# Moving the 1024-column sum of weight blocks in paired w_out from VectorE to GpSimd

## What is computed

```python
for layer in range(DEPTH):
    h = rms_norm(x, norm_w[layer])
    proj = jnp.einsum('bsd,de->bse', h, w_in[layer])
    ...                      # four token mixers: GLA, sliding window, differential, RG-LRU
    y = jnp.concatenate([y_gla, y_swa, y_diff, y_lru], axis=-1)
    y = y * jax.nn.silu(gate)
    x = x + jnp.einsum('bse,ed->bsd', y, w_out[layer])
```

## Time and profile before

| | us |
|---|---|
| median of 3 runs | 2874.45 |
| lowest, highest | 2874.27, 2875.07 |
| the profiled execution | 2875.7 |
| its span, first to last instruction | 2874.0 |

### The profile page before, as it was taken

One profiled execution on the slowest core, in us unless ns is written; L12 is line 12 of the kernel. 1 busy time (PEld: TensorE's weight loads), 2 busy tenths in 40 slices (PEclk: granted clock), 3 DMA queues, 4 the chain that ended last, 5 costly groups with the idle time before them and its releaser, 6 DMA issues.

```text
span 2874.0 us, 35012 instructions
## 1 busy us (share of the span) xinstructions
PE 2860.9 (100%) x13317; PEld 2346.7 (82%) x13317; DVE 1837.1 (64%) x2428; ACT 1519.7 (53%) x2125; POOL 54.5 (2%) x90
## 2 busy tenths in 40 slices
PE   9999999999999999999999999999999999999999
PEld 7878888888888888888888788888888888888887
DVE  6545555555666568888864455555556665688888
ACT  6444445545556556555644345455556565564454
POOL 2000000000000000000000000000000000000000
PEclk9999999999999999999999999999999999999999
DMA  8655555666555665666676555565656556656665
GB/s 252 197 169 164 173 175 179 188 186 180 174 170 167 214 190 185 221 224 216 202 216 184 176 169 169 177 187 178 187 177 179 168 168 214 190 187 224 233 220 176
DMA packets 282873, 546.51 MB, mean 190 GB/s; under 512 B 17528, under 2 KB 22272, under 8 KB 282704
## 3 DMA queue, kind: packets, MB, share of 16 engines
q1 hardware_dynamic: 272848, 525.40, 59.0%
q0 software_dynamic: 5168, 16.73, 1.9%
q10 hardware_dynamic: 4688, 2.13, 0.3%
HBM read 535.81 MB, written 8.39 MB: 189 GB/s over the span
## 4 chain that ended last, share of the span: by engine, by line
PE 97%; DVE 1%; DMA 1%; issue 1%; ACT 0%; SPq 0%; DVEq 0%; ACTq 0%
PE main L1346 79%; PE mixer L1346 16%; DMA w_raw<-in_w_out 1%; PE mixer L1629 0%; DVE w_lo L839 0%; PE mixer L1387 0%; PE mixer L1376 0%; DVE mix L1119 0%; PE mixer L1565 0%; PE mixer L1608 0%; DVE w_lo L822 0%; ACT w_hi L598 0%; DMA w_raw<-in_w_in 0%; PE mixer L1593 0%; PE mixer L1481 0%
## 5 line engine op out<-in xcount | busy, mean ns | idle before, releaser
L1346 PE MATMUL main<-w_hi,act 128*128 128x512 f32 x6624 | 2134.7, 394 | 4.3 <-DVE act L811 1.4
L1346 PEld LDWEIGHTS main<-w_hi,act 128*128 128x128 f32 x6624 | 1244.7, 188 | 275.1 <-DVE w_lo L822 7.4
L822 DVE TENSOR_TENSOR w_lo<-w_raw,w_hi 128x1024 fp32r<-128x1024 f32 x736 | 895.1, 1228 | 758.4 <-ACT w_hi L457 754.5
L1346 PE MATMUL main<-w_lo,act 128*128 128x512 f32 x3312 | 1290.9, 390 | 0.0
L457 ACT ACTIVATE w_hi<-w_raw 128x1024 fp32r<-128x1024 f32 x736 | 770.6, 1057 | 559.1 <-PE main L1346 509.5
L1346 PEld LDWEIGHTS main<-w_lo,act 128*128 128x128 f32 x3312 | 623.2, 188 | 123.1
L598 ACT ACTIVATE w_hi<-w_raw 128x1024 fp32r<-128x1024 f32 x256 | 268.1, 1056 | 202.8 <-DVE w_raw L836 56.9
L839 DVE TENSOR_TENSOR w_lo<-w_raw,w_hi 128x1024 fp32r<-128x1024 f32 x256 | 307.9, 1220 | 34.5 <-ACT w_hi L598 30.6
L1346 PE MATMUL mixer<-w_hi,act 128*128 128x512 f32 x736 | 239.9, 389 | 0.0
L1346 PEld LDWEIGHTS mixer<-w_hi,act 128*128 128x128 f32 x736 | 138.1, 188 | 28.5
L1346 PE MATMUL mixer<-w_lo,act 128*128 128x512 f32 x368 | 143.2, 389 | 0.0
(11 more groups left out here) (267 smaller groups left out, 1667.4 us busy)
## 6 DMA issues: line engine op xcount, KB each, us to landing
w_raw<-in_w_in SPq DMA_DIRECT2D x736, 512.0 KB, 3.8
w_raw<-in_w_out SPq DMA_DIRECT2D x256, 512.0 KB, 4.3
out<-mix POOLq DMA_DIRECT2D x7, 1024.0 KB, 5.7
mix<-in_x POOLq DMA_DIRECT2D x4, 1024.0 KB, 6.8
mix<-out POOLq DMA_DIRECT2D x4, 1024.0 KB, 8.1
mix_Y<-in_x SPq DMA_DIRECT2D x7, 512.0 KB, 6.7
act_T<-in_lru_w_r ACTq DMA_DIRECT2D x16, 64.0 KB, 1.8
act_T<-in_lru_w_i ACTq DMA_DIRECT2D x16, 64.0 KB, 1.9
```

Of the source, the lines that this page charges most:

```text
L822: dve.tensor_tensor(w_lo[:, n % LO, :, :], w_raw[:, n % RAW, :, :], w_hi[:, n % HI, :, :].bitcast(F32), ALU.subtract).then_inc(w_lo_ready, 1)
L1346: return pe.matmul(out_, lhsT, rhs, start=start, stop=stop, skip_group_check=True)
```

## The change

L846 is taken out of VectorE's program and given to GpSimd as `block_sums`. GpSimd waits for the even block's landing and for b_raw[0] (b_sum at 2u + 2, u numbering the 48 fast places), makes the sum and raises b_pair. ScalarE's b_hi waits for b_pair, and for SP a fast place's even buffer is free when its own w_lo is made and b_pair is raised (`first_half`), in place of the wait for the odd slot's w_lo. On GpSimd the order of loads and stores of x changes: x pairs 0 and 1 are loaded ahead, a store comes at the start of the next x pair, and the load of x pair c + 1 behind the first sum of x pair c.

```diff
--- before.py
+++ after.py
@@ -206,7 +206,7 @@
         X_BANKS = (M[0], M[1], M[2], M[5])
         c_ready, p_done, p_added = sem("c_ready"), sem("p_done"), sem("p_added")
         s_sum, s_hi, s_ready = sem("s_summed"), sem("s_hi_ready"), sem("s_ready")
-        b_sum = sem("b_summed")
+        b_sum, b_pair = sem("b_summed"), sem("b_pair_summed")
         b_hi_ready, b_lo_ready, b_used = sem("b_hi_ready"), sem("b_lo_ready"), sem("b_used")
 
         block = ctx.enter_context(nc.Block())
@@ -254,10 +254,11 @@
 
         P_STEPS = 8
 
-        def read_raw(n):
-
-            s = n % (CHUNKS * NG) - J_OUT * NG
-            return n + 2 if s >= 0 and s % 2 == 0 and is_fast(s % 32) else n + 1
+        def first_half(n):
+
+            layer, s = divmod(n, CHUNKS * NG)
+            c, s = divmod(s - J_OUT * NG, 2 * NG)
+            return fast_number(layer, c, ORDER[s // 2]) if c >= 0 and s % 2 == 0 and is_fast(s) else None
 
         def y_scale(layer, k):
             return par[:, layer, Q_YS + k:Q_YS + k + 1]
@@ -278,7 +279,10 @@
                     col = (j - J_OUT + g % 2) * NC
                     src = w_out[layer, rows, col:col + NC]
                 if n >= RAW:
-                    sp.wait_ge(w_lo_ready, read_raw(n - RAW))
+                    sp.wait_ge(w_lo_ready, n - RAW + 1)
+                    u = first_half(n - RAW)
+                    if u is not None:
+                        sp.wait_ge(b_pair, u + 1)
                 sp.dma_start(w_raw[:, n % RAW, :, :], src.rearrange("(k p) n -> p k n", p=P)
                              ).then_inc(w_landed[n % RAW], 16)
 
@@ -388,6 +392,15 @@
                 pool.dma_start(out[0, :, 2 * c * NC:(2 * c + 2) * NC].rearrange("(t p) n -> p t n", p=P), x_pair[f % 2]
                                ).then_inc(x_stored, 16)
 
+            def block_sums(layer, c, g):
+
+                u = fast_number(layer, c, g)
+                n = pair_group(layer, c, 2 * ORDER.index(g))
+                pool.wait_ge(w_landed[n % RAW], 16 * (n // RAW + 1))
+                pool.wait_ge(b_sum, 2 * u + 2)
+                pool.tensor_tensor(b_raw[:, 1:3, :], w_raw[:, n % RAW, :, :],
+                                   b_raw[:, 0:1, :].to_broadcast([P, 2, NC]), ALU.add).then_inc(b_pair, 1)
+
             pool.wait_ge(w_used, 6)
             def rows(dst, src):
                 pool.dma_start(dst, src).then_inc(rows_in, 16)
@@ -410,11 +423,16 @@
                 for i in range(4):
                     mask_intra(layer, i)
                 load_x(layer, 0)
+                load_x(layer, 1)
                 for c in range(PAIRS):
-                    if c + 1 < PAIRS:
-                        load_x(layer, c + 1)
-                    if layer < LAST or c + 1 < PAIRS:
-                        store_x(layer, c)
+                    if c:
+                        store_x(layer, c - 1)
+                    for q, g in enumerate(FAST):
+                        block_sums(layer, c, g)
+                        if q == 0 and 0 < c < PAIRS - 1:
+                            load_x(layer, c + 1)
+                if layer < LAST:
+                    store_x(layer, PAIRS - 1)
                 if layer < LAST:
                     f = (layer + 1) * PAIRS
                     pool.wait_ge(x_stored, f * 16)
@@ -594,10 +612,10 @@
                 fast = is_fast(s) and s % 2
                 if fast:
                     u = fast_number(layer, c, ORDER[s // 2])
-                    act.wait_ge(b_sum, 3 * u + 1)
+                    act.wait_ge(b_sum, 2 * u + 1)
                 act.activation(w_hi[:, n % HI, :, :], w_raw[:, n % RAW, :, :], ACT.Copy).then_inc(w_hi_ready, 1)
                 if fast:
-                    act.wait_ge(b_sum, 3 * u + 3)
+                    act.wait_ge(b_pair, u + 1)
                     act.wait_ge(b_used, u)
                     act.activation(b_hi[:, :, :], b_raw, ACT.Copy).then_inc(b_hi_ready, 1)
 
@@ -839,12 +857,9 @@
                 dve.tensor_tensor(w_lo[:, n % LO, :, :], raw, w_hi[:, n % HI, :, :].bitcast(F32),
                                   ALU.subtract).then_inc(w_lo_ready, 1)
                 if fast and s % 2 == 0:
-                    dve.wait_ge(b_sum, 3 * u + 1)
+                    dve.wait_ge(b_sum, 2 * u + 1)
                     dve.wait_ge(b_used, u)
                     dve.tensor_tensor(b_raw[:, 0, :], second[:, 0, :], second[:, 1, :], ALU.subtract).then_inc(b_sum, 1)
-                    dve.wait_ge(b_sum, 3 * u + 2)
-                    dve.tensor_tensor(b_raw[:, 1:3, :], raw, b_raw[:, 0:1, :].to_broadcast([P, 2, NC]),
-                                      ALU.add).then_inc(b_sum, 1)
                 if fast and s % 2:
                     dve.wait_ge(b_hi_ready, u + 1)
                     dve.tensor_tensor(b_lo[:, :, :], b_raw, b_hi[:, :, :].bitcast(F32), ALU.subtract).then_inc(b_lo_ready, 1)
```

## The result

| | before | changed |
|---|---|---|
| median | 2874.43 us (4 runs) | 2949.97 us (4 runs) |
| lowest, highest | 2874.27, 2875.07 | 2949.64, 2951.11 |
| span of the profiled execution | 2874.0 | 2948.1 |
| ratio | | 1.0263 [1.0245, 1.0281] |

A forecast was written before the change was run, and what follows sets the result against it. TensorE was taken to bound the kernel (97% of the chain). Per x pair, first lateness plus periods' excess over 10.2 us minus slack summed to 64.2, less 2.6 existing waits: 62 us slower, 2936.5 us, range 2886 to 2972.

The forecast's parts named there:

- Step (b): Paired w_out fast places: GpSimd's sum takes 2.3 us, waits for the odd w_lo and ends 2.1 us later than before.
- Rival 1: Fast places: GpSimd does not wait for VectorE, the sum ends at 4.8, total 2889 us; chance 0.14.
- Step (c): Fast-place period: work queued behind the late sum makes it 11.3 us, 1.1 over TensorE's; 13.1 with an x load.
- rival 4: x load and both weights start together: perhaps 1 to 2 us more in four places, 4 to 8 us; no chance given.
- The move costs nothing else: Reordered x loads and stores: no cost beyond the x load's meeting with the weights, since their waits are done by then.
- The slack is won back between x pairs: Between x pairs of paired w_out: TensorE's lead of b_lo over its use recovers, as in the kernel before.
- waits already there: Paired w_out: 2.6 us that TensorE's weight loads already wait for b_lo, taken off the summed 64.2 us.
- ten regular places: Stretch between x pairs: said to be long enough to win the slack back.
- step d: x pair 0 of each layer, x pair 3 of layer 0: VectorE's split operations add 1.6 us a period.
- first lateness: First fast place of each x pair: the sum, and b_lo behind it, comes 2.1 us later.

The follow-up runs named there:

- e2: Changed kernel with VectorE's odd w_lo held back until GpSimd's sum is done; 2919.05 us, ratio 1.0147.
- e4: Changed kernel with the sum split, VectorE making the first 512 of 1024 columns and GpSimd the other 512; 2886.39 us, ratio 1.0038.
- e9: Changed kernel with the next regular slot's w_hi made before b_hi on ScalarE and its w_lo before b_lo on VectorE; 2936.56 us, ratio 1.0208.
- e10: e9 with, in addition, SP asking for the odd weight block of the next fast place first; 2904.08 us, ratio 1.0101.
- e13: Changed kernel with only the two weight loads of a fast place swapped, odd block first; 2940.80 us, ratio 1.0228.
- e1: Kernel before with only GpSimd's changed order of x loads and stores, the sum staying on VectorE; 2883.40 us, ratio 1.0022.
- e3: Kernel before with the 1024-column sum made twice in a row on VectorE; 2932.03 us, ratio 1.0192.
- e11: Kernel before with VectorE's three sums ahead of the even w_lo and the even block's successor asked for early; 2872.12 us, ratio 0.9985.
- e12: Kernel before with SP asking for the even block's successor when the sum is done, not the odd w_lo; 2873.82 us, ratio 0.9992.
- e5: Changed kernel with the load of the next x behind the last sum of an x pair, not the first; 2950.31 us, ratio 1.0261.

## Why the prediction was right, and where it missed

**Step (b), the sum's end: right.** I put it at 5.77 behind L836; it came at 5.80. GpSimd's work was 2.25 us behind the wait (taken: 2.2) and 2.40 alone (2.3); the odd w_lo started first, kept its 1.22 and held GpSimd up, as the earlier trace rows had shown. Rival 1 (no wait) needed 4.8. The sum was recorded from 0.23 behind the odd w_lo, where I had said 0.04 to 0.1, and with 3.24 us, just under the 3.3 to 3.4. e2, e4 and the reverse case in the changed kernel confirm the mechanism on both sides.

**Step (c), the period: right for plain ones, 11.3 and 11.30.** The bound was VectorE's queue, and the landing at about 10.8 lay just under it, as e9, e10 and e13 show. With an x load I took 13.1; the changed kernel has 13.70, 13.63, 13.77 and 13.96. The step's size was off by 0.5 to 0.9 in four places, 2.7 us: load and weights now start together, which is rival 4's case. I had priced it at 1 to 2 us a place, too high, and not put it into the sum.

**"The move costs nothing else": wrong.** The forecast did have the load meet the weights in x pairs 1 and 2 of layer 1, at 2.9 us each; e1, with the sum still on VectorE, has 2.3 and 2.6 there. What it did not have is that x pairs 2 and 3 then begin 1.1 and 2.7 us late. I argued from what each load waits for, and not from what it pushes back. My range for e1 left out even the part that the forecast had.

**The slack is won back between x pairs: wrong, above all in layer 1.** From the last fast place of one x pair to the last of the next, TensorE's first b_hi load fell further behind the kernel before by (us):

| | x pair 0 | 1 | 2 | 3 |
|---|---|---|---|---|
| layer 0, forecast | 8.7 | 7.0 | 7.0 | 13.6 |
| layer 0, measured | 7.5 | 8.5 | 8.8 | 11.7 |
| layer 1, forecast | 8.7 | 7.0 | 7.0 | 5.2 |
| layer 1, measured | 7.5 | 10.5 | 10.8 | 9.0 |

The measured ones add up to 74.2, the forecast's to 64.2, less 2.6 that I took off for waits already there. Errors of both signs are in it: x pair 0 of both layers and x pair 3 of layer 0 came out 4 us lower than forecast in all, the other five 14 us higher, and 11 of these lie in three x pairs of layer 1. I had used 2.4 us, the slack of x pair 1 of layer 0, for x pairs 1 and 2 of both layers and for x pair 3 of layer 1. The kernel before has next to no slack in x pair 1 of layer 1:

```profile
2637.93 1.76 DVE L850 TENSOR_TENSOR b_lo<-mix_Y,b_hi 128x1536 fp32r<-128x1536 f32 x1 [0.42 <-ACT b_hi L602]
```

```profile
2639.74 0.19 PEld L1346 LDWEIGHTS mixer<-b_hi,sums 128*128 128x128 f32 x1 [0.44 <-DVE b_lo L850]
```

b_lo ends at 2639.69, and TensorE has waited 0.44 us for it. In x pair 2 of layer 1 it is the same (0.05 us from b_lo's end to the load), and in x pair 3 the slack is 1.44. With these three values the forecast would have been 5.7 us higher; the x loads account for 1.5 more.

The sentence on the "ten regular places" that win the slack back is wrong too. Ten blocks lie there, which are five regular places (14, 15, 0, 1 and 2). With one fast place they are 47 products, and at 10.20 / 15 = 0.68 us each TensorE needs 31.96 us, which is the shortest that any run has there in layer 1. From the last fast place of one x pair to the first of the next the changed kernel takes 34.27, 35.24 and 35.38 us in layer 1, the kernel before 32.36, 32.80 and 31.96. The reorder of the loads is not needed for this: e3, which has the old order and a late sum, takes 34.51, 35.01 and 35.12. In that stretch VectorE of the changed kernel (x pair 1 to 2) stands idle for a landing:

```profile
2771.09 0.69 DVE L854 TENSOR_TENSOR w_raw<-w_raw 128x512 f32<-128x512 f32 x1 [4.95 <-DMA w_raw<-in_w_out]
```

TensorE has no transposes of x to make there in layer 1 (in layer 0 there are sixteen, L1387 in the kernel before, which its chain shows as two pieces of 0.87 us), so the weights' side, with a store of 1 MB beside its reload, has less time to recover: TensorE's own time there is 33.77 us in layer 0 and 31.96 in layer 1 (e11, e12). That these 1.8 us are the reason for the difference between the layers is argued, and was not tried; the rest of the 11 us stays open.

**Splits (step d): right in mechanism, high in effect.** Periods with splits were 12.9 (11.3 + 1.6). In x pair 3 of layer 0 GpSimd came before the odd w_lo in the first fast place, so the sum ended there 4.95 behind L836 and the first lateness was 0.9 less; TensorE's 1.0 us of waits in the kernel before make the rest of the 2 us. In x pair 0 VectorE's first period was 12.70, but TensorE's was 11.33, since b_lo was still 1.6 us ahead of its use in the first fast place.

The Trainium skill had both halves: half of VectorE's rate for a two-input operation (GPSIMD Engine Reference, "3.1 Elementwise — side-by-side cycle accounting"; measured 2.40 us against VectorE's 1.23, a ratio of 1.95), and the mutual exclusion (SBUF — State Buffer, "Who interferes with whom"), which the records of 3.24, 2.76 and 2.31 us agree with.

## What to carry to other kernels

That an engine has idle time is no reason to give it a step from the middle of a loop: what counts is when the step ends, and what is queued behind those who wait for it. Write the loop as a period, with one sum for each chain that closes it (the engine's queue, the buffer's reload), and compare each with the bound engine's own period; here they were 9.2 us for VectorE's queue and 9.8 for the reload, against TensorE's 10.2, and a step made 2.1 us later turned 1.0 us of room in the queue into 1.1 us of loss, in each of the 40 periods. If one bound is lifted and the time hardly follows, look for the second one just below it, as in e9 and e10.

## What the runs showed that I had not expected

The granted clock of TensorE fell in six short stretches of the changed kernel, all within or right behind its waits for b_lo. Windows around the first (us; busy times of PE, PEld, DVE, ACT, POOL with counts; granted clock; DMA share; GB/s):

```profile
1322.00:1326.20 4.20, 1.08 (x5) 0.60 (x4) 2.35 (x2) 3.51 (x4) 0.30 (x1) 1.00 0.63 215
1326.20:1329.60 3.40, 3.40 (x9) 2.65 (x8) 3.40 (x5) 1.94 (x2) 0.00 (x0) 0.50 0.63 191
1329.60:1335.00 5.40, 5.40 (x25) 4.41 (x25) 1.81 (x3) 1.35 (x2) 3.25 (x1) 1.00 0.35 109
```

TensorE had waited 3.5 us for b_lo, began again at 1325.66, and from 1326.20 to 1329.60 was granted 0.50, that is 1.2 in place of 2.4 GHz: nine matmuls, 0.43 us from one weight load to the next in place of 0.23. The longest such stretch was 6.8 us, at 2698.3. It seems to cost little here, since TensorE would have waited for its operands anyway: the period from L836 to L836 is 11.37 behind the first and 11.78 behind the longest, in place of 11.31. Not every wait of this length has one: TensorE waited 3.6 us before 1232.3, and the granted clock stayed at 1.00. e5, e9, e10 and e13 have three to five such stretches each; the kernel before and e1 to e4 have none in paired w_out while TensorE works.
